# Linear attention's output with tokens on partitions: states as the moving operand, the norm along the free side

## The reference

```
within(c)  = mask(q_c k_c^T) v_c                        # tokens of the same chunk
add(c)     = kd_c^T v_c                                  # what chunk c adds, 64 x 128
state(c)   = decay(c) * state(c - 1) + add(c)            # 16 chunks, forward and backward
o_c        = within(c) + q_c state(c - 1)                # both directions summed
y          = rmsnorm(o, over the 128 values) * norm_g * silu(gate)
out        = concat(y_na, y) @ w_out
```

## Time and profile before

| | us |
|---|---|
| median of 3 runs | 3255.03 (3254.58 to 3259.12) |
| the profiled execution | 3260.14 |
| its span in the trace | 3258.3 |
| mean granted clock of TensorE | 0.981 |
| PE busy | 3142.3 (96%) |
| DVE busy | 1476.7 (45%) |
| ACT busy | 1211.8 (37%) |
| the GLA output stage, 2378.69 to 2447.10 | 68.4 |

### The profile page before, as it was taken

The page is one execution under the profiler, slowest core; times in us unless marked ns, Lnnn a source line. Parts: engine busy times, 40 slices in busy tenths (PEclk is TensorE's granted clock), DMA queues, the critical chain, the costliest instruction groups (busy, mean ns, idle before and its releaser), DMA issues.

```text
span 3258.3 us, 42926 instructions
## 1 busy us (share of the span) xinstructions
PE 3142.3 (96%) x16966; PEld 2572.4 (79%) x16966; DVE 1476.7 (45%) x2223; ACT 1211.8 (37%) x1840; POOL 395.3 (12%) x616
## 2 busy tenths in 40 slices
PE   7999998999999999999999999999999999999997
PEld 5888887788778878888888778557788788888886
DVE  5662357666653435525534532555444322223233
ACT  3552138876663232212212331565353321212121
POOL 0110007655542000000000000120000000000000
PEclk9999998999999999999999999999989999999999
DMA  3222220000004211111111131001002111111111
GB/s 137 72 77 81 106 84 8 2 1 2 1 1 156 89 40 52 45 52 45 51 45 52 45 127 52 14 1 39 33 14 91 45 52 45 51 45 51 46 50 67
DMA packets 48121, 168.54 MB, mean 52 GB/s; under 512 B 6784, under 2 KB 7936, under 8 KB 47600
## 3 DMA queue, kind: packets, MB, share of 16 engines
q1 hardware_dynamic: 37008, 126.49, 11.4%
q0 software_dynamic: 10976, 40.15, 3.5%
HBM read 144.07 MB, written 16.78 MB: 49 GB/s over the span
## 4 chain that ended last, share of the span: by engine, by line
PE 90%; ACT 4%; DVE 3%; issue 2%; POOL 0%; DMA 0%; DVEq 0%; ACTq 0%; SPq 0%; POOLq 0%
PE PS L224 70%; PE PS L853 3%; PE PS L839 3%; PE PS L238 3%; PE PS L824 2%; PE PS L823 2%; PE PS L1576 1%; PE PS L1603 1%; PE PS L1588 1%; ACT PT L932 1%; PE PS L874 1%; ACT P_SHORT L922 1%; PE PS L282 1%; PE PS L865 1%; DVE PT L1021 1%
## 5 line engine op out<-in xcount | busy, mean ns | idle before, releaser
L197 ACT CAST WHI<-RAW 128x1024 fp32r<-128x1024 f32 x220 | 231.4, 1052 | 1368.5 <-PE PS L224 1348.4
L202 DVE TENSOR_TENSOR WLO<-RAW,WHI 128x1024 fp32r<-128x1024 f32 x220 | 269.8, 1227 | 1011.0 <-ACT WHI L197 1010.5
L224 PE MATMUL PS<-HLO,WHI 128*128 128x512 f32 x2176 | 673.4, 391 | 0.0
L224 PEld LDWEIGHTS PS<-HLO,WHI 128*128 128x128 f32 x2176 | 410.7, 189 | 86.0
L224 PE MATMUL PS<-X_HI,WHI 128*128 128x512 f32 x1520 | 473.4, 393 | 4.5 <-DVE W L333 2.2
L224 PE MATMUL PS<-X_HI,WLO 128*128 128x512 f32 x1520 | 470.0, 391 | 0.0
L224 PEld LDWEIGHTS PS<-X_HI,WHI 128*128 128x128 f32 x1520 | 285.5, 189 | 67.6 <-DVE W L333 2.7
L224 PEld LDWEIGHTS PS<-X_HI,WLO 128*128 128x128 f32 x1520 | 286.7, 189 | 59.8
L224 PE MATMUL PS<-HID_HI,WHI 128*128 128x512 f32 x864 | 267.2, 391 | 5.0 <-DVE HID_LO L1313 5.0
L224 PE MATMUL PS<-HID_LO,WHI 128*128 128x512 f32 x864 | 266.8, 390 | 0.0
L224 PE MATMUL PS<-HID_HI,WLO 128*128 128x512 f32 x864 | 266.6, 390 | 0.0
(11 more groups left out here) (328 smaller groups left out, 4663.1 us busy)
## 6 DMA issues: line engine op xcount, KB each, us to landing
RAW<-in_w SPq DMA_DIRECT2D x220, 512.0 KB, 3.2
X<-in_x SPq DMA_DIRECT2D x8, 512.0 KB, 8.7
Q<-QN POOLq DMA_DIRECT2D x32, 128.0 KB, 2.7
merged<-W POOLq DMA_DIRECT2D x8, 512.0 KB, 3.1
W<-gate POOLq DMA_DIRECT2D x8, 512.0 KB, 4.0
W<-merged POOLq DMA_DIRECT2D x8, 512.0 KB, 4.7
X<-in_x POOLq DMA_DIRECT2D x8, 512.0 KB, 10.1
x_kept<-X POOLq DMA_DIRECT2D x8, 512.0 KB, 7.8
```

Of the source, the lines that this page charges most:

```text
L197: nc.scalar.copy(WHI[:, slot, :], RAW[:, slot, :]).then_inc(w_hi, 1)
L202: nc.vector.tensor_tensor(WLO[:, slot, :], RAW[:, slot, :], WHI[:, slot, :].bitcast(F32), ALU.subtract).then_inc(w_lo, 1)
L224: last = nc.tensor.matmul(o[:, half], w[:, slot, cols], x(k)[:, half], start=(k == 0 and w is WHI and x is hi), stop=(k == kcs - 1 and w i ...
```

## The change

The output of a head now has tokens on partitions and values along the free side, and the norm is computed in that layout:

- `across` swaps its operands: 64 tokens of `QDEC` are the weights (64 x 64), 128 columns of `SST` the moving side. The two directions write different halves of the partitions, and which chunks belong to a turn is changed accordingly. `within` swaps as well (both sides are 128 x 128).
- The sum of squares is a DVE reduction of `OSQ` into `OSUM` ([128, 8]: one number per token), Ln and Exp work on 8 columns, and DVE multiplies the output, read from PSUM, by the result into `ON`.
- PE transposes `ON` back (8 transposes per head) into the same PSUM place; DVE multiplies by norm weight and gate in one operation, into `RG`; high and low part are made from that.
- There are three state tiles. PE forms the contributions of heads 1 and 2 ahead of across(0), and those of head 3 right behind it. ACT copies three heads' contributions first, head 3's behind the Square of head 0. DVE scans heads 0 and 1 first, head 2 behind the sum of head 0, head 3 behind the sum of head 1.
- One semaphore is used for two things (`gl_exp` is folded into `gl_ln`), which makes room for `gl_turned`.

```diff
-    SST = [sb(f"SST{i}", [P, N_CH], g_at + 8 * KB * i) for i in range(2)]
+    SST = [sb(f"SST{i}", [P, N_CH], g_at + 8 * KB * i) for i in range(3)]
...
-                nc.tensor.matmul(SIDE[h % 2][:, tok], VG[:, t, h, :], AMT[h][:, t, :],
+                nc.tensor.matmul(SIDE[h % 2][:, P * t:P * t + P], AMT[h][:, t, :], VG[:, t, h, :],
                                  start=(t % 4 == 0), stop=False)
...
-                    c, b = 8 * turn + x, 8 - 8 * turn + x
+                    c, b, stop = 2 * x + turn, 2 * x + 1 - turn, turn == 1 and x % 4 == 3
                     if c:
-                        last = nc.tensor.matmul(SIDE[h % 2][:, 64 * c:64 * c + 64], SST[h % 2][fwd, :, c - 1],
-                                                QDEC[h][fwd, 64 * c:64 * c + 64], start=False, stop=(turn == 1 and x == 7))
+                        last = nc.tensor.matmul(SIDE[h % 2][64 * turn:64 * turn + 64, P * x:P * x + P],
+                                                QDEC[h][fwd, 64 * c:64 * c + 64], SST[h % 3][fwd, :, c - 1],
+                                                start=False, stop=stop)
...
-        def mean(h):
-            pe.wait_ge(gl_sq, h + 1)
-            halves(pe, SIDE[h % 2], ONES[:, :], OSQ).then_inc(gl_ms, 1)
+        def turn_back(h):
+            pe.wait_ge(gl_rs, h + 1)
+            for t in range(QT):
+                last = nc.tensor.transpose(SIDE[h % 2][:, P * t:P * t + P], ON[:, t, :], IDENT[:, :])
+            last.then_inc(gl_turned, 1)
 
         contributions(0)
         within(0)
+        contributions(1)
+        contributions(2)
         for h in range(GLA_HEADS):
-            if h + 1 < GLA_HEADS:
-                contributions(h + 1)
             across(h)
+            if h + 3 < GLA_HEADS:
+                contributions(h + 3)
             if h + 1 < GLA_HEADS:
                 within(h + 1)
-            mean(h)
+            turn_back(h)
...
     def act_gla(act):
-        act_gla_copies(act, 0)
+        for h in range(3):
+            act_gla_copies(act, h)
         for h in range(GLA_HEADS):
...
+            nc.scalar.activation(OSQ[:, :, :], SIDE[h % 2].rearrange("p (t v) -> p t v", v=P), ACT.Square)\
+                .then_inc(gl_sq, 1)
+            if h + 3 < GLA_HEADS:
+                act_gla_copies(act, h + 3)
             act.wait_ge(gl_ms, h + 1)
+            nc.scalar.activation(ORS[:, h, :], OSUM[:, h, :], ACT.Ln, scale=1.0 / GLA_DV, bias=EPS_T[:, 0:1])\
+                .then_inc(gl_root, 1)
+            act.wait_ge(gl_root, 2 * h + 1)
+            nc.scalar.activation(ORS[:, h, :], ORS[:, h, :], ACT.Exp, scale=-0.5).then_inc(gl_root, 1)
...
+    def dve_gla_norm(dve, h):
+        dve.wait_ge(gl_root, 2 * h + 2)
+        if h:
+            dve.wait_ge(gl_turned, h)
+        nc.vector.tensor_tensor(ON[:, :, :], SIDE[h % 2].rearrange("p (t v) -> p t v", v=P),
+                                ORS[:, h, :].unsqueeze(2).to_broadcast([P, QT, P]), ALU.mult).then_inc(gl_rs, 1)
+
+    def dve_gla_gate(dve, h):
+        dve.wait_ge(gl_turned, h + 1)
         dve.wait_ge(rg_done, h + 1)
+        nc.vector.scalar_tensor_tensor(RG[h][:, :], SIDE[h % 2], NG[:, 0:1], RG[h][:, :], ALU.mult, ALU.mult)\
+            .then_inc(gl_y, 1)
...
         dve_gla_states(dve, 0)
+        dve_gla_states(dve, 1)
         for h in range(GLA_HEADS):
-            if h + 1 < GLA_HEADS:
-                dve_gla_states(dve, h + 1)
-            dve_gla_out(dve, h)
+            dve_gla_sums_of_squares(dve, h)
+            if h + 2 < GLA_HEADS:
+                dve_gla_states(dve, h + 2)
+            dve_gla_norm(dve, h)
+            if h:
+                dve_gla_lo(dve, h - 1)
+            dve_gla_gate(dve, h)
+        dve_gla_lo(dve, GLA_HEADS - 1)
```

More of the change, by code:

```diff
@@ L1753, in act_gla_logs @@
         act.wait_ge(gl_abs, h + 1)
-        nc.scalar.activation(KINV[h][:, :], KINV[h][:, :], ACT.Exp, scale=-1.0).then_inc(gl_exp, 1)
-        act.wait_ge(gl_exp, h + 1)
+        nc.scalar.activation(KINV[h][:, :], KINV[h][:, :], ACT.Exp, scale=-1.0).then_inc(gl_ln, 1)
+        act.wait_ge(gl_ln, 2 * h + 1)
         nc.scalar.activation(KINV[h][:, :], KINV[h][:, :], ACT.Ln, bias=1.0).then_inc(gl_ln, 1)
@@ L1926, in across @@
                     if b < N_CH - 1:
-                        last = nc.tensor.matmul(SIDE[h % 2][:, 64 * b:64 * b + 64], SST[h % 2][bwd, :, N_CH - 2 - b],
-                                                QDEC[h][bwd, 64 * b:64 * b + 64], start=False, stop=(turn == 1 and x == 7))
+                        last = nc.tensor.matmul(SIDE[h % 2][64 - 64 * turn:128 - 64 * turn, P * x:P * x + P],
+                                                QDEC[h][bwd, 64 * b:64 * b + 64], SST[h % 3][bwd, :, N_CH - 2 - b],
+                                                start=False, stop=stop)
@@ L1955, in act_gla @@
         for h in range(GLA_HEADS):
-            if h + 1 < GLA_HEADS:
-                act_gla_copies(act, h + 1)
             act.wait_ge(gl_o, 2 * h + 2)
-            if h >= 2:
-                act.wait_ge(gl_lo, h - 1)
-            nc.scalar.copy(OY[h % 2][:, :], SIDE[h % 2])
             if h:
-                act.wait_ge(gl_root, h)
-            nc.scalar.activation(OSQ[:, :], SIDE[h % 2], ACT.Square).then_inc(gl_sq, 1)
+                act.wait_ge(gl_ms, h)
+            nc.scalar.activation(OSQ[:, :, :], SIDE[h % 2].rearrange("p (t v) -> p t v", v=P), ACT.Square)\
+                .then_inc(gl_sq, 1)
@@ L1970, in act_gla @@
-            act.wait_ge(gl_root, h + 1)
-            nc.scalar.activation(ORS[:, :], ORS[:, :], ACT.Exp, scale=-0.5).then_inc(gl_hi, 1)
-            act.wait_ge(gl_y, h + 1)
-            nc.scalar.copy(OG_HI[:, h, :], OY[h % 2][:, :]).then_inc(gl_hi, 1)
+                act_gla_hi(act, h - 1)
+        act_gla_hi(act, GLA_HEADS - 1)
     def dve_gla_states(dve, h):
-        sst = SST[h % 2]
+        sst = SST[h % 3]
         dve.wait_ge(gl_zero, GLA_HEADS + N_CH + 1 + h + 1)
```

43 lines of the change are left out of this document (19 added, 24 removed).

## The result

| | before | after |
|---|---|---|
| median of 16 runs each | 3256.35 (3254.33 to 3261.71) | 3265.64 (3261.58 to 3273.32) |
| ratio after / before, 95% interval | | 1.0026 [1.0019, 1.0033] |
| the profiled execution and its span | 3260.14, 3258.3 | 3266.71, 3264.9 |
| the stage, first contribution to first record of the output projection | 68.4 | 76.0 |
| PE busy and idle in the stage | 64.3, 4.1 | 55.2, 20.8 |

The changed kernel is slower by 0.26%, 6 to 11 us. The stage grew by 7.6 us. Across the rest of the program little moved: the stage begins 0.7 us earlier in the trace (2378.01 against 2378.69), and from its end to the end of the last instruction there are 811 us in both.

What follows compares the result with a forecast made beforehand. TensorE bounds the kernel; only the 68.4 us linear-attention output stage changes. Per-head chains sum to 77.6 to 84.8, taken 80.9: 12.5 more, plus 0.5 for the clock, +13 on 3255.03 gives 3268; own range 3264 to 3274, wide range 3250 to 3284.

Steps and rivals of the forecast that it cites:

- Across with operands swapped: Products with the states on PE: strided moving reads cost double per element, 0.22 us a pair, 7.1 a head, no gain.
- 0.43 a pair: Rival in across: strided moving reads paid in both passes, 13.5 us a head, 3294 in all; chance 0.15.
- Cheap moving reads: Rival in across: strided moving reads not slower; 3249 at full clock, mixed around 3258, up to 3266; chance 0.23.
- Contributions of heads 1 and 2 ahead of across 0: On PE's queue: across 0 starts at 2391.2 instead of 2388.9, 2.3 us lost, and ends at +19.7.
- The ring of the norm: Square, sum, Ln, Exp, table loads and multiplication off PE: 5.5 us a head; PE waits 3 to 5.
- Ahead of the norm: Head 3's copies on ACT delay head 0's norm, 8.4 to 10 us; head 3's scans on DVE delay head 1's, 6.9.
- Head 0's upper end of 40.5: Latest end of across 1, after head 0's norm and transposes: +38.4 to 40.5 us from the first contribution, before +33.7.
- The mis-sized term: the transposes: Eight transposes a head on PE: 1.9 us at full clock, up to 3.6 at half.
- its own sign: Test set beforehand: across at 7.1 us a head with the stage still short means the ACT and DVE ring was mis-sized.
- the ring on ScalarE and VectorE: Work on ACT and DVE around the norm, such as copies, scans, sum, Ln, Exp and multiplication; the norm itself 5.5 us.
- The clock: PE idles more, so the granted clock stays low; 0.5 us more at the start of the output projection.

Runs made afterwards that it cites:

- e1: Changed kernel with across reading its 128 moving state columns side by side (not the states of one chunk, only the price kept): 3257.4 us, ratio 1.0000.
- e6: Changed kernel with running ahead undone on all engines, contributions, copies and scans of head h+1 again ahead of across(h): 3267.9 us, ratio 1.0026 to the kernel before.
- e7: Changed kernel with each head's transposes behind the next head's across, and head 3's scans behind head 0's multiplication: 3256.8 us, ratio 0.9998 to the kernel before.
- e8: Changed kernel with head 3's transposes moved into the output projection, between its fourth and fifth slice: 3258.5 us, ratio 1.0003 to the kernel before.
- e5: Changed kernel with head 3's scans on VectorE moved from between head 1's sum and multiplication to behind head 0's multiplication: 3263.7 us, ratio 1.0015 to the kernel before.
- e12: Changed kernel with transposes behind the next head's across, head 3's scans behind head 0's norm, head 3's transposes inside the output projection: 3252.7 us, ratio 0.9985.
- e2: Kernel before with across loading its 128 weight columns of the state tile side by side (not the states of one chunk): 3254.8 us, ratio 0.9989.
- e10: Kernel before with head 3's two ones-matmuls moved into the output projection, between its second and third slice: 3257.8 us, ratio 0.9997.
- e4: Kernel before with states stored chunk by chunk, 16 dependent VectorE steps a head instead of two scans: 3249.5 us, ratio 0.9975.
- e11: Kernel before with states stored chunk by chunk and head 3's two ones-matmuls moved into the output projection: 3246.9 us, ratio 0.9966.
- e3: Changed kernel with states stored chunk by chunk, dependent VectorE steps instead of two scans a head: 3258.1 us, ratio 1.0000 to the kernel before.

## Why the prediction was right

Forecast slower, 3268 at a stage of 80.9; measured 3265.6 at 76.0.

- **Across with operands swapped.** 0.22 a pair and 7.1 us a head were said, 0.217 and 6.7 to 7.0 came. The reason given (about twice the price for elements 64 bytes apart, taken over from the weights to the moving side) is what the two side-by-side runs show. That the price did not come twice within one record (0.43 a pair) nothing in the profile before could tell; there the forecast chose by likeness, and was lucky to that extent. Both records of a product pay it, 0.217 against 0.109 a pair, as both loads did before. Cheap moving reads would have given 67.0 in the stage and no change in time, as e1 shows: that rival's "around 3258" was its measured 3257.4, so it fell on its premise and not on its size.
- **Contributions of heads 1 and 2 ahead of across 0.** End of across 0 at +19.7 said, +19.3 measured. The loss is real in place (12.3 us against 10.3 in e6), but undoing it gains nothing, since the contributions come back elsewhere on PE's queue, at a lower clock.
- **The ring of the norm.** 5.5 us said, 5.5 measured (2446.61 to 2452.08). That PE waits for it was the main step, and e7 and e8 show it by taking it away: 9 us (2 of them by the scans' order) and 7. The waits, 3.5 to 5.9 us, came where the forecast had looked for 3 to 5.
- **Ahead of the norm.** Across 1 ends at +37.4 (38.4 to 40.5 said), across 2 16.8 us later (17.3 to 19.0), across 3 14.4 later (14.5 to 16.2), tail 7.45 (7.4 to 9.1). All lie at or under the lower ends, which together with across 0 were 1.6 us too long. The largest part is head 0's, 0.6: head 3's copies began 1.0 us behind the end of across 0, right behind Square, and not 1.7, since the contributions had started beside across's last records. That head 3's scans stand on head 1's chain is confirmed by e5. Head 0's upper end of 40.5 does not follow from its terms, which give 40.0.
- **The mis-sized term: the transposes.** I read the earlier trace rows, sixteen records in 1.91 us, as one head's eight transposes and so as 1.9 us at full clock, and bounded the half clock with the 3.78 of sixteen records of within. A product of float32 is two records, but a transpose is one: the rows after show x8 per head. The sixteen records were two heads'. Eight take 0.95 to 1.09 us at the full clock (e8, e12) and 1.97 at the half. So the true range was 1.0 to 2.0 a head, and the half clock, which I had put at 3.6, gave my lower end. Heads 1 to 3 had this range (head 0's were put at 1.9 alone), and taking 80.9, near the middle, cost 0.7 to 0.8 us in each, 2.2 of the 4.9 us by which the stage was forecast too long; the contributions at low clock that I had allowed for (up to 1.6, about half of it taken, 0.7) did not come either, since contributions(3) ran at 1.00. With the 1.6 of the lower ends that is nearly all. By its own sign (across as said and the stage short) the forecast would have blamed the ring on ScalarE and VectorE; the ring had the size said, and it was this term.
- **The clock.** I expected more idling to lower it. In the stage it rose from 0.76 to 0.85. Of 34.1 us at the half clock in the stage and just behind it, 23.9 are left. That did not enter the sum much, as within and across were not what ended last, but it kept the tail from getting worse: the projection began at 0.96, not below the 0.92 of the earlier trace rows, where I had put 0.5 us on.

The forecast of 3268 stands on a median of 3255.03; beside the change the same kernel took 3256.35. So the 2.4 us between forecast and time hide 3.7 in the difference: 13 said, 9.3 came, of which 12.5 and 7.6 in the stage. The other 1.3 are the luck of a baseline that came out higher. The 1.7 that the medians moved beyond the stage is within the interval of the ratio.

## What to carry to other kernels

When a norm moves from a matrix product to the vector engines, count what the matrix engine waits for, not what it is relieved of: here 9 us of its work went and 17 us of waiting came. Then look in the order of that engine for work already due that can stand in front of such a wait. Here moving the transposes behind the next head's across (with one move of the scans), and the last ones into the next stage, took 12.9 us off, more than the 9.3 that the change had cost. In the kernel before, filling the tail in the same way gave nothing, since the chain behind the moved work was as long as its cover. And before choosing which operand is stationary, look at the distance between its elements: a layout chosen for a scan was paid for on either side of the product.

Count the records of an operation before pricing it by a row: is it one or two per instruction, and one head's or two?

## What the runs showed of the hardware

- Float32 elements 64 bytes apart in SBUF: 128 moving columns take 391 ns a record instead of 269 (after, e1), a load of 128 columns 307 instead of 188 (before, e2); a pair of records 0.217 us instead of 0.109 at 2.4 GHz, and at 1.2 GHz 0.217 instead of 0.213. Such a read goes no faster at 2.4 GHz than at 1.2. The memory rule of 16-byte lines (the Trainium skill, SBUF — State Buffer, Specifications (TRN2)) agrees in direction with the rows at 2.4 GHz; it gives no price for TensorE, and these are the prices.
- In the kernel before, the granted clock fell to 1.2 GHz four times in the stage, 1.7 to 5.8 us into an across, three of them with PE busy without a wait since the head before. With the change it fell four times too, three of them in a wait and one in the transposes right behind one, never in an across: head 0's ran at 1.00 throughout against 0.63, with PE as busy in both. So within, which comes next, took 2.05 us against 3.3 to 3.8. It goes with weights that are read 64 bytes apart: only before and e10 have them, and in each of the two the clock fell three times with PE busy for 22 us and more since its last wait of over 0.2 us. In the twelve other traces, whose weights lie side by side, every fall in the stage came in a wait or at most 2.6 us behind one (among these are falls in an across of e4, e6, e8 and e11). Why strided weights should do it is not shown.
- A chain of dependent operations on 128 x 128 elements costs VectorE 0.37 us each; 14 of them and one more in two halves take 5.9 us (e3) where two scans over the same data take 4.47.
- Work that comes right behind a wait of PE mostly ran slower here, down to half as fast: contributions 5.0 instead of 3.3 (e6), transposes 1.97 instead of 0.95. It is no rule: in e8 head 2's transposes came behind a wait of 3.5 us and ran at 1.00, in 1.09 us. Filling the last wait gave more than its length in the traces (6.8 for 5.5, e8).
